# Token order meta, samples, prompt in a one-core hybrid decoder layer: the 16 meta tokens are left out of queries, gates, attention output, mixing and feed-forward

## The reference, cut to what is computed

```python
x  = layer_norm(concat([meta, x_prompt]), ln_in_g, ln_in_b)      # 528 tokens; the 8 samples in the same way
q, k, v, qi, wi, ki, hq, hf, hi, hg = split(x @ w_in)            # 2048 -> 6728 columns
# group A: top-k of an indexer over qi, ki, wi, then attention of q over the kept k, v (ALiBi, GQA)
# group B: HGRN2 recurrence: S_t = diag(f_t) S_{t-1} + (1 - f_t) i_t^T ; o_t = S_t^T silu(q_t)
#          then RMSNorm per head and the gate silu(hg)
x  = layer_norm(ALPHA * x + concat([attn_o, hg_o]) @ w_out, ln1_g, ln1_b)
x  = layer_norm(ALPHA * x + (silu(x @ w_gate) * (x @ w_up)) @ w_down, ln2_g, ln2_b)    # 2048 -> 5632 -> 2048
y_prompt = x[:, 16:]
return y_prompt, y_sample, k_prompt, v_prompt, kidx_prompt, hgrn_prompt, k_sample, v_sample, kidx_sample, hgrn_sample
```

## Time and profile before

| | |
|---|---|
| runs (us) | 2887.70, 2894.63, 2897.01; median 2894.63 |
| profiled execution, first to last instruction | 2888.6 us |
| its time beside the span | not recorded; the median of the runs is 6.0 us above its span, the fastest run 0.9 us below |
| TensorE matmul (PE) busy | 2770.1 us (96%) |
| TensorE weight load (PEld) busy | 2698.6 us (93%), overlapping PE |
| VectorE (DVE) busy | 1256.3 us (43%) |
| ScalarE (ACT) busy | 802.6 us (28%) |
| GpSimd (POOL) busy | 198.8 us (7%) |
| DMA | 243.6 MB, mean 84 GB/s |

### The profile page before, as it was taken

How to read it: one execution, slowest core, us unless ns; L and a number is a source line. 1 busy time by engine, 2 the same in 40 slices (tenths; PEclk the granted TensorE clock), 3 DMA queues, 4 the chain that set the end, 5 groups by cost and what they waited for, 6 DMA issues and landing times.

```text
span 2888.6 us, 49681 instructions
## 1 busy us (share of the span) xinstructions
PE 2770.1 (96%) x21603; PEld 2698.6 (93%) x21603; DVE 1256.3 (43%) x1846; ACT 802.6 (28%) x1222; POOL 198.8 (7%) x214
## 2 busy tenths in 40 slices
PE   5999999999999999889999999999999999999996
PEld 5989999999998889889999999999999999999995
DVE  5156777667566314562323232323232323232337
ACT  5243444432334212242111111121111121212124
POOL 1111112110000220120000000000000000000002
PEclk9899999999998978989999999999999999999998
DMA  4323333323221322312323232323232323232321
GB/s 128 98 59 89 89 88 87 87 76 92 68 67 63 95 89 65 87 45 92 94 80 92 85 89 88 88 89 88 89 88 88 88 88 88 85 92 81 94 76 60
DMA packets 341223, 243.60 MB, mean 84 GB/s; under 512 B 7208, under 2 KB 310616, under 8 KB 340504
## 3 DMA queue, kind: packets, MB, share of 16 engines
q1 hardware_dynamic: 333696, 218.97, 26.1%
q0 software_dynamic: 7344, 21.80, 2.6%
HBM read 229.43 MB, written 11.31 MB: 83 GB/s over the span
## 4 chain that ended last, share of the span: by engine, by line
PE 93%; DVE 4%; ACT 2%; issue 1%; DMA 0%; SPq 0%; DVEq 0%; ACTq 0%
PE acc L1098 81%; PE b L1084 2%; PE acc L1120 1%; DVE lnd L2038 1%; PE b L1370 1%; PE b L1246 1%; PE b L1453 1%; PE b L1340 1%; DVE wl L1554 1%; PE b L1262 1%; ACT wh L596 1%; PE b L1275 1%; PE b L1431 1%; PE b L1371 0%; PE b L1455 0%
## 5 line engine op out<-in xcount | busy, mean ns | idle before, releaser
L1098 PE MATMUL acc<-xh,wh 128*128 128x268 f32 (+1 forms) x4896 | 1038.9, 294 | 37.9 <-issue 25.0
L1098 PE MATMUL acc<-xl,wh 128*128 128x268 f32 (+1 forms) x4896 | 1015.0, 289 | 0.0
L1098 PE MATMUL acc<-xh,wl 128*128 128x268 f32 (+1 forms) x4896 | 1012.3, 288 | 0.0
L1554 DVE TENSOR_TENSOR wl<-raw,wh 128x2048 fp32r<-128x2048 f32 (+1 forms) x201 | 462.6, 2302 | 1030.3 <-ACT wh L596 1012.3
L1098 PEld LDWEIGHTS acc<-xh,wh 128*128 128x128 f32 (+1 forms) x4896 | 774.1, 191 | 47.9 <-issue 27.9
L1098 PEld LDWEIGHTS acc<-xl,wh 128*128 128x128 f32 (+1 forms) x4896 | 777.9, 191 | 0.0
L1098 PEld LDWEIGHTS acc<-xh,wl 128*128 128x128 f32 (+1 forms) x4896 | 773.3, 191 | 0.0
L596 ACT ACTIVATE wh<-raw 128x2048 fp32r<-128x2048 f32 x200 | 382.7, 1914 | 1285.3 <-PE acc L1098 1282.1
L1098 PE MATMUL acc<-hh,wh 128*128 128x268 f32 x1408 | 287.9, 285 | 3.0 <-DVE hl L2063 2.2
L1098 PE MATMUL acc<-hh,wl 128*128 128x268 f32 x1408 | 287.8, 286 | 0.0
L1098 PE MATMUL acc<-hl,wh 128*128 128x268 f32 x1408 | 287.5, 285 | 0.0
(11 more groups left out here) (401 smaller groups left out, 2026.6 us busy)
## 6 DMA issues: line engine op xcount, KB each, us to landing
raw<-in_w_in_dram SPq DMA_DIRECT2D x52, 1024.0 KB, 5.7
raw<-in_w_gate_dram SPq DMA_DIRECT2D x44, 1024.0 KB, 5.5
raw<-in_w_up_dram SPq DMA_DIRECT2D x44, 1024.0 KB
raw<-in_w_down_dram SPq DMA_DIRECT2D x44, 1024.0 KB, 5.0
raw<-in_w_out_dram SPq DMA_DIRECT2D x16, 1024.0 KB, 5.4
xtok<-in_x_prompt_dram SPq DMA_DIRECT2D x4, 1024.0 KB, 9.0
ss<-in_state_hgrn_dram POOLq DMA_DIRECT2D x8, 512.0 KB, 4.7
out_dram<-ss POOLq DMA_DIRECT2D x8, 512.0 KB, 3.9
```

The source lines that it names most:

```text
L1098: ins = mm(acc[0:rows, t.odd, half, 0:HALF], a, b[:, kx0 + k, half * HALF:half * HALF + HALF], start=(k == 0 and n == 0), stop=(k == kt - ...
L1554: V.tensor_tensor(wl[:, s.odd, 0:n], raw[:, s.odd, 0:n], fr(wh[:, s.odd, 0:n]), ALU.subtract)\
```

## The change

The tokens are ordered meta, samples, prompt: meta at 0 to 15, samples at 16 to 23, prompt from 24. S0 = 16 is the first token that reaches y. `product` gets an argument lo: with lo = M0 = 0 it computes all 536 tokens (two halves of 268), with lo = S0 the last 520 (two halves of 260, LIVE). The slots wk, hf, hi, k and v keep lo = 0; qi, hq, hg, q, both parts of the mixing, gate, up and down take lo = 16. `two_products` takes 260 always.

VectorE, ScalarE and GpSimd work on the slice S0:NT wherever a tile is such a result. The meta queries' small work is dropped: four matmul places (L1240, L1272, L1343, L1374), the transposes of lgm, and about a dozen small VectorE and ScalarE instructions per group or head. `ke` is multiplied on GpSimd in two pieces instead of one, and the piece of `et` for meta is gone, so GpSimd issues as many instructions as before. No DMA is added, removed or resized; the two that load the sample and meta tokens write other partitions.

```diff
-M0 = NS
-R0 = NS + NM
+M0 = 0
+S0 = NM
+R0 = NM + NS
 HALF = NT // 2
+LIVE = (NT - S0) // 2
...
+    def alive(t):
+        return acc[:, t.odd, :, 0:LIVE]
+    HG_FROM = (M0, S0, M0, S0)
...
-            pt(et[:, off:off + NM], et[:, off:off + NM], kf[:, M0:R0], ALU.mult)
-            pt(ke[:, M0:NT], ke[:, M0:NT], kf[:, M0:NT], ALU.mult)
+            pt(ke[:, R0:NT], ke[:, R0:NT], kf[:, R0:NT], ALU.mult)
+            pt(ke[:, M0:S0], ke[:, M0:S0], kf[:, M0:S0], ALU.mult)
...
-        def product(s, t, kt, width, sub, x, between, rows=P, kx0=0):
+        def product(s, t, kt, width, sub, x, between, rows=P, kx0=0, lo=S0):
+            n_ = (NT - lo) // 2
...
-                        ins = mm(acc[0:rows, t.odd, half, 0:HALF], a, b[:, kx0 + k, half * HALF:half * HALF + HALF],
+                        ins = mm(acc[0:rows, t.odd, half, 0:n_], a, b[:, kx0 + k, lo + half * n_:lo + half * n_ + n_],
...
-                            ins = mm(acc[:, t_.odd, half, 0:HALF], a, b[:, k, half * HALF:half * HALF + HALF],
+                            ins = mm(acc[:, t_.odd, half, 0:LIVE], a, b[:, k, S0 + half * LIVE:S0 + half * LIVE + LIVE],
...
-        product(At(4), At(4), KD, 72, 0, X, {3: (lambda: kx_turn(6),), 8: (lambda: kx_turn(7),)}, rows=72)
+        product(At(4), At(4), KD, 72, 0, X, {3: (lambda: kx_turn(6),), 8: (lambda: kx_turn(7),)}, rows=72, lo=M0)
...
-            off = NB * (32 + 64 + 96 + 128)
-            mm(b5[0:NM, 3 * P:3 * P + NM], et[:, off:off + NM], qd[:, M0:R0], start=True, stop=True)\
-                .then_inc(sem("head_turned"), 1)
...
-            mm(b5[:, M0:R0], itok[0:NM, 4, :], aTm[:], start=True, stop=True)
...
-                product(s, s, KD, P, 0, X, late(h - 1, j))
+                product(s, s, KD, P, 0, X, late(h - 1, j), lo=HG_FROM[j])
...
-                if i == 0:
-                    last = mm(b6[0:NM, 2 * NM + NM * hd:3 * NM + NM * hd], q[:, hd, M0:R0], k[:, M0:R0],
-                              start=True, stop=True)
...
-                if i == 0:
-                    last = turn(b6[0:NM, 2 * P + NM * hd:2 * P + NM * hd + NM], lgm[:, hd, :])
...
-            if i == 0:
-                for hd in range(2):
-                    last = mm(b7[:, 2 * P + NM * hd:2 * P + NM * hd + NM], v[0:NM, 4, :],
-                              pTm[:, 2 * P + NM * hd:2 * P + NM * hd + NM], start=True, stop=True)
...
-                product(s, s, KD, P, 0, X, side)
+                product(s, s, KD, P, 0, X, side, lo=M0 if j < 2 else S0)
...
-                            V.tensor_tensor(cut(sacc[:, m, :]), cut(sacc[:, m, :]), whole(t_), ALU.add)\
+                            V.tensor_tensor(cut(sacc[:, m, S0:NT]), cut(sacc[:, m, S0:NT]), alive(t_), ALU.add)\
```

More of the change, by code:

```diff
@@ L199, in program @@
     pT = rb.take("pT", [P, 2, NR])
-    pTm = rb.take("pTm", [NM, 2 * P + 2 * NM])
-    lgm = rb.take("lgm", [NM, 2, NM])
+    pTm = rb.take("pTm", [NM, 2 * P])
     nmx = rb.take("nmx", [P, 2, 2])
-    nmxm = rb.take("nmxm", [NM, 2, 2])
     distS = rb.take("distS", [NS, KEEP_S + 1])
@@ L872, in att_exp @@
                                       accum_out=nmx[:, 1, hd:hd + 1])
-                if i == 0:
-                    last = act.activation(lgm[:, hd, :], lgm[:, hd, :], ACT.Exp, bias=nmxm[:, 0, hd:hd + 1],
-                                   accum_out=nmxm[:, 1, hd:hd + 1])
             last.then_inc(sem("att_exp"), 1)
@@ L1221, in idx_scores @@
                 mm(real_[:, 0:w], a, kiT[64 * e:64 * e + 64, R0:R0 + w], start=True, stop=True)
-                last = mm(meta[:, 0:NM], a, kiT[64 * e:64 * e + 64, M0:R0], start=True, stop=True)
+                last = mm(meta[:, 0:NM], a, kiT[64 * e:64 * e + 64, M0:S0], start=True, stop=True)
             last.then_inc(sem("idx_scores"), 1)
@@ L1321, in kv_turn @@
             if small:
[L1322 to L1323 removed]
+                turn(b7[0:NM, 0:P], src[:, M0:S0])
+                last = turn(b7[0:NS, P:2 * P], src[:, S0:R0])
             else:
@@ L1541, in _ @@
                     else:
-                        last = turn(out[0:NS], sacc[:, 4 * q + k, 0:NS])
+                        last = turn(out[0:NS], sacc[:, 4 * q + k, S0:R0])
                 last.then_inc(sem("y_turned"), 1)
@@ L1866, in attend @@
                                           in1=keepmask[:, WOFF[i]:WOFF[i] + w], op0=ALU.mult, op1=ALU.add))
-                if i == 0:
-                    ch(V.scalar_tensor_tensor(out=lgm[:, hd, :], in0=dist[0:NM, 400:400 + NM], scalar=slope,
-                                              in1=causal[0:NM, 0:NM], op0=ALU.mult, op1=ALU.add))
             dve.wait_ge(sem("att_scores"), n + 1)
@@ L1940, in add_mix @@
             dve.wait_ge(sem("mm"), (t + 1).v)
-            V.tensor_tensor(cut(sacc[:, m, :]), cut(sacc[:, m, :]), whole(t), ALU.add).then_inc(sem(f"acc_read{t.odd}"), 1)
+            V.tensor_tensor(cut(sacc[:, m, S0:NT]), cut(sacc[:, m, S0:NT]), alive(t), ALU.add).then_inc(sem(f"acc_read{t.odd}"), 1)
         def sample_att(b):
@@ L1989, in finish @@
             dst = tile_of(sacc, m)
-            V.tensor_tensor(cut(dst), cut(dst), whole(t), ALU.add).then_inc(sem("s_done"), 1)
+            V.tensor_tensor(cut(dst), cut(dst), alive(t), ALU.add).then_inc(sem("s_done"), 1)
             dve.wait_ge(sem("s_done"), (m + 1).v)
@@ L2017, in ln_stats @@
             dve.wait_ge(sem("ln_sums"), n)
-            for src, part in ((b4, slice(R0, NT)), (b5, slice(0, R0))):
+            for src, part in ((b4, slice(R0, NT)), (b5, slice(S0, R0))):
                 last = V.tensor_scalar(mu[:, part], src[:, 0:part.stop - part.start], 1.0 / D, None, ALU.mult)
```

213 lines of the change are left out of this document (95 added, 118 removed).

## The result

The changed kernel takes 2787.32 us (median of 4 runs, 2777.86 to 2790.04). The kernel before took 2893.40 us beside it (4 runs, 2887.70 to 2897.01). The ratio is 0.962, 95% interval 0.959 to 0.965: 106 us or 3.7% faster. The profiled execution of the changed kernel took 2790.04 us, its span is 2788.5 us, 100.1 us less than the span before. The medians are 106.1 us apart: the profiled execution of before has a span 4.8 us under its median, that of after one 1.2 us over it.

What follows compares the result with a forecast made beforehand. TensorE was taken as the bound, at matmuls times the distance between their starts. Savings of 57.8 + 0.8 + 6.7 + 2.0 - 0.6 = 66.7 us took 2894.6 us to 2828 us, range 2806 to 2862 us.

Steps and rivals of the forecast that it cites:

- Products: TensorE's matmuls in all stages: 16,512 go from 268 to 260 columns and save 3.5 ns each, 57.8 us.
- fixed reading: Products: the 12 ns above columns over clock are fixed for each matmul, so 8 columns less save 3.3 ns.
- Pauses: Feed-forward loop branch: the sequencer's lead of some 17 pairs is worth less, 0.6 us lost over ten branches (0 to 3).
- Half clock: Mixing stage from 890 us: some 250 matmuls at half clock save 3.2 ns more each, 0.8 us (0 to 1).
- Meta queries' work: Heads and groups: the dropped small matmul passes of L1240, L1272, L1343, L1374 and lgm save 6.7 us (5 to 10).
- Elementwise: Second and third norms, where TensorE waits: steps on 520 instead of 536 columns save 2.0 us (0.5 to 4).
- Blocks of 64 bytes (1): Products: SBUF is read in whole blocks, so the gain is 1 ns a matmul, 25 us in all, 2869 us; chance 0.07.
- a fixed pace of a pair (2): Products: 123.5 ns a pair whatever the width; only small work and norms gain, 9 us, 2886 us; chance 0.07.
- a loss by the starts (3): Products: moving rows at new starts collide with weight rows, 2 ns lost a matmul, +24 us, 2919 us; chance 0.04.
- a wait per slot (4): Heads: VectorE or ScalarE waits replace part of the saving, 8 us, 2836 us; chance 0.82 together with the forecast.

Runs made afterwards that it cites:

- width experiment: The changed kernel with all products back at 268 columns a half, from tokens 0 and 268, the meta queries' work still left out: 2860.11 us, 0.988 of before.
- the linear table: Changed kernel with other columns in the feed-forward products alone: 264 took 121.56 ns a matmul, 256 took 117.65; the kernel before, with 268, 123.20.

## Why the prediction was right in kind and too small

- **Products, 57.8 us (range 43 to 73).** Right in mechanism: columns set the pace, neither the weight load nor the sequencer. It measured 4.02 ns instead of 3.5 in the feed-forward, and 16,512 x 4.02 = 66.4 us. The fixed reading was right (3.24 ns), and the new starts gave 0.78 ns, about the 0.7 ns that I had allowed at the end, a size without a known cause. The width experiment gives 72.8 us. The 6.4 us beyond 66.4 are open: the half clock doesn't explain them, since the mean granted clock of the two kernels' runs is the same (0.976), and 3 us of them are not in the profiled executions. The prediction also set 114.2 ns beside the trace from a formula of the Trainium skill; the section that it cites gives that formula for a matmul by itself and other figures for a stream with weight loads, so it was no price for this stream.
- **Pauses, -0.6 us (0 to -3).** The step that failed. "At the loop branch the sequencer stands 3.4 us while the array eats its lead" put both pauses down to the lead, as if the change could only alter the lead. The second was the wait for the next piece of code, and the change moved the loop so that it went: 10.2 us of "issue" in the profiled executions, 12.9 us of the feed-forward at equal columns; 15.5 us in all by the kernel before with 40 small matmuls, 22 us by the changed kernel with 24. My own rows showed it: 12 matmuls, then a second pause.
- **Half clock, 0.8 us (0 to 1).** This term failed with it. It counted only what matmuls in D1 save at half clock, and took the length of the half clock as given, at nothing and without a reason. The mean granted clock of the runs rose from 0.970 to 0.976, which by the rate above is an estimate of some 14 us, spread over the second pause, the meta queries' work and chance.
- **Meta queries' work, 6.7 us (5 to 10).** Mis-sized: 16.3 us. About 8 us of it are the clock's by the estimate above, and the other 8 are inside the range. By stage the heads gave 4.3 for 3.7 us, and the groups and D1 11.7 us instead of 3, of which the 6.9 us of D1 are half clock.
- **Elementwise, 2.0 us.** The add took 694 ns instead of 711, 17 ns less and in line with the 21 ns allowed. But the norms gave next to nothing: the stage of `two_products` 1.1 us, of which products are 192 x 4.0 ns = 0.8, and the tail is 1.0 us longer.
- **Rivals.** Blocks of 64 bytes (1) fell by the linear table; a fixed pace of a pair (2) and a loss by the starts (3) fell by 119.18 ns; a wait per slot (4) is in no row of the waits.

The parts come near the whole: 72.8 us for columns and starts, 15.5 us for the second pause and 16.3 us for the meta queries' work make 104.6 us, each from a kernel of its own, of 106.1 us measured. That they meet within 2 us is partly luck, since by their intervals the last two are uncertain by some 6 us each. The terms come to 66.7 us in the forecast; the missing 38 are 14 of the products (58.6 forecast with their half clock), 16 of the pauses and 10 of the meta queries, less the 2 of the norms. My range took the bounds of the products and gave the other terms together 14 us at most (their upper bounds add up to 15), so a term of 15 us that stood there as a loss could not fit in.

## What to carry to other kernels

Count the pauses behind a hardware loop's branch one by one, and ask what code each waits for. If there are two, an edit that adds or drops a few instructions anywhere ahead of the loop can be worth 15 to 36 us over nine branches, of either sign, and the same edit with a few dozen harmless instructions beside it tells that from its own effect. Count the code as it stands, with what lies in a loop once, and not the instructions executed. Compare the granted clocks of two kernels' runs as well: here 0.001 went with 2.6 us. Where the code is small enough, write the busiest engine's loop out (20 us here). And a change of width should be priced by columns over clock with the fixed part left alone, and with a nanosecond for what the new starts may do.

## What the runs showed of the hardware that I had not expected

- A fetch of code is 16.4 KB, and TensorE stood twice behind a branch, 1.3 to 1.5 us in the chain each time, where the second pause came 12 pairs (24 instructions) after the first; by the theory that is how far the loop's start lies ahead of a piece's end. With four instructions more in front it came after 10 pairs and brought the half clock behind every branch: 2909.8 us against 2873.7 us for the same work with its code 160 instructions on.
- A matmul of 256 to 268 float32 columns costs its columns at 2.4 GHz plus 10.8 to 12.1 ns, and the start columns decide within that: 119.18, 119.96 and 120.41 ns for 260 columns. At the half clock nothing is on top.
- Less work can be slower without any new wait for data: the kernel before without one block's meta attention lost 15 us, by the place of its code.
- One and the same code between two stages took 192.9 us in one trace and 205.4 us in another, at granted clocks of 0.93 and 0.87.
